# Attention weights transposed in 32x32 blocks by VectorE and placed by SBUF transfers

## The reference

```python
u = einsum('bsd,dc->bsc', rmsnorm(x, g), w_in)       # q, k, v, gates of three branches
ya = forgetting_attention(qa, ka, va, log_f) * silu(za)   # 4 heads, causal, decay bias
yb = dilated_mixture_attention(rope(qb), rope(kb), vb) * silu(zb)   # 6 heads
yc = banded_attention(rope(qc), rope(kc), vc, 127, sinks) * silu(zc) # 6 query, 2 kv heads
merged = sigmoid(ga)*(ya@w_br_a) + sigmoid(gb)*(yb@w_br_b) + sigmoid(gc)*(yc@w_br_c)
x = x + merged @ w_out
```

## Time and profile before

| | us |
|---|---|
| median of 3 runs | 2319.72 |
| lowest and highest | 2318.62, 2319.8 |
| profiled execution | 2318.26 |
| its span, first to last instruction | 2316.5 |
| TensorE busy | 2300.3 (99%) |
| VectorE busy | 1282.9 (55%) |
| ScalarE busy | 855.2 (37%) |

### The profile page before, as it was taken

The page is one execution under the profiler, slowest core; times in us unless marked ns, Lnnn a source line. Parts: engine busy times, 40 slices in busy tenths (PEclk is TensorE's granted clock), DMA queues, the critical chain, the costliest instruction groups (busy, mean ns, idle before and its releaser), DMA issues.

```text
span 2316.5 us, 28465 instructions
## 1 busy us (share of the span) xinstructions
PE 2300.3 (99%) x11494; PEld 1877.6 (81%) x11494; DVE 1282.9 (55%) x2217; ACT 855.2 (37%) x1419; POOL 13.9 (1%) x14
## 2 busy tenths in 40 slices
PE   9999999999999999999999999999999999999998
PEld 7787778878777787878889888888888888888887
DVE  5855565556656556586545544444755546444445
ACT  5334443433444334354334432232322334332233
POOL 0000000000000000200000000000000000000000
PEclk9999999999999999999999999999999999999999
DMA  4322222322322233324224222222222212222221
GB/s 174 93 87 86 80 78 99 105 78 92 91 82 76 82 102 109 121 70 139 91 82 129 99 92 97 95 92 99 91 93 99 91 46 92 99 91 99 92 93 63
DMA packets 67271, 218.23 MB, mean 94 GB/s; under 512 B 8479, under 2 KB 11167, under 8 KB 67012
## 3 DMA queue, kind: packets, MB, share of 16 engines
q1 hardware_dynamic: 67140, 216.41, 28.2%
HBM read 209.02 MB, written 3.42 MB: 92 GB/s over the span
## 4 chain that ended last, share of the span: by engine, by line
PE 96%; DVE 2%; ACT 1%; POOL 0%; issue 0%; DMA 0%; SPq 0%; POOLq 0%; DVEq 0%; ACTq 0%
PE ps L370 27%; PE ps L372 27%; PE ps L371 27%; PE ps L573 2%; PE ps L661 2%; PE ps L396 2%; PE ps L397 2%; PE ps L398 2%; PE ps L641 1%; PE ps L1457 1%; PE ps L1407 1%; PE ps L462 1%; POOL t_UP L170 0%; PE ps L923 0%; PE ps L921 0%; PE ps L922 0%
## 5 line engine op out<-in xcount | busy, mean ns | idle before, releaser
L370 PE MATMUL ps<-t_P0H,t_whi 128*128 128x512 f32 x1664 | 670.8, 403 | 1.9 <-DVE t_P0L L176 1.9
L372 PE MATMUL ps<-t_P0H,t_wlo 128*128 128x512 f32 x1664 | 655.8, 394 | 0.0
L371 PE MATMUL ps<-t_P0L,t_whi 128*128 128x512 f32 x1664 | 654.6, 393 | 0.0
L182 ACT ACTIVATE t_whi<-t_raw 128x1024 fp32r<-128x1024 f32 (+3 forms) x395 | 404.9, 1029 | 418.8 <-PE ps L372 346.4
L173 DVE TENSOR_TENSOR t_wlo<-t_raw,t_whi 128x1024 fp32r<-128x1024 f32 (+3 forms) x394 | 468.1, 1188 | 52.5 <-PE ps L398 35.0
L370 PEld LDWEIGHTS ps<-t_P0H,t_whi 128*128 128x128 f32 x1664 | 313.2, 188 | 93.7 <-issue 23.0
L372 PEld LDWEIGHTS ps<-t_P0H,t_wlo 128*128 128x128 f32 x1664 | 312.6, 188 | 72.9
L371 PEld LDWEIGHTS ps<-t_P0L,t_whi 128*128 128x128 f32 x1664 | 313.1, 188 | 69.7 <-issue 2.4
L370 PE MATMUL ps<-t_P1H,t_whi 128*128 128x512 f32 (+1 forms) x932 | 361.3, 388 | 0.3 <-DVE t_P1L L173 0.3
L371 PE MATMUL ps<-t_P1L,t_whi 128*128 128x512 f32 (+1 forms) x932 | 359.5, 386 | 0.0
L372 PE MATMUL ps<-t_P1H,t_wlo 128*128 128x512 f32 (+1 forms) x916 | 355.6, 388 | 0.0
(11 more groups left out here) (241 smaller groups left out, 2403.5 us busy)
## 6 DMA issues: line engine op xcount, KB each, us to landing
t_raw<-in_wts SPq DMA_DIRECT2D x362, 512.0 KB, 3.4
t_raw<-in_wts SPq DMA_DIRECT2D x16, 384.0 KB, 3.0
t_raw<-in_wts SPq DMA_DIRECT2D x13, 256.0 KB, 2.7
t_raw<-in_wts SPq DMA_DIRECT2D x4, 520.0 KB, 4.9
t_X<-in_xT SPq DMA_DIRECT2D x8, 256.0 KB, 5.6
t_TMX<-t_TMX SPq DMA_DIRECT2D x28, 64.0 KB, 2.0
t_TMP<-t_TMX SPq DMA_DIRECT2D x24, 64.0 KB, 2.0
outT<-t_X SPq DMA_DIRECT2D x4, 384.0 KB, 2.6
```

The lines of the kernel that those rows point to most:

```text
L182: return lambda e: e.activation(o, a, f, **k)
L370: e.matmul(bank[:, 0:N], wh, xh, start=first, stop=False)
L371: e.matmul(bank[:, 0:N], wh, xl, start=False, stop=False)
L372: return e.matmul(bank[:, 0:N], wl, xh, start=False, stop=end)
```

## The change

In the first block turn is replaced by turn_by_dma. VectorE transposes all 32x32 blocks of a head's weights in one instruction and writes them sorted, so that for every partition group i the blocks that belong to partition group j lie side by side. Twelve transfers issued by SP move the blocks with i and j different (32 partitions, 192 or 256 values each), and ScalarE copies the four with i = j. Both heads of a unit share these. The products read the operand as four runs of 32 and lag the scores by three units instead of two. Each stage lends one buffer more for the sources (a part of M or QKV that is idle then). The two banks of the transposes become score banks, four in all; TB shrinks to two buffers, the temporaries to nine; two semaphores more are there for the transfers.

```diff
-NRAW, NHI, NLO, NTMP, NTMX = 4, 4, 3, 5, 5
+NRAW, NHI, NLO, NTMP, NTMX = 4, 4, 3, 5, 4
...
-    SB = Turns([ps[:, b, :] for b in (3, 4)])
-    PTP = Turns([ps[:, 5, :]])
+    SB = Turns([ps[:, b, :] for b in (3, 4, 5)])
+    PTP = Turns([])
...
-    TB = Turns([T["Tb"][:, i, :] for i in range(3)] + [T["TbX"][:, 0, :]])
-    PTS = Turns([T["PTb"][:, i, :] for i in range(2)])
+    TB = Turns([T["Tb"][:, 0, :], T["TbX"][:, 0, :]])
+    PTS = Turns([])
...
+    blocks = Turns([wide(T["Tb"][:, 1:3, :])])
+    turned = Turns([wide(T["PTb"][:, :, :]), wide(T["PTX"][:, :, :])])
+    moved = [0]
...
+        def turn_by_dma(u):
+            kh = u["cols"] // 128
+            run_ = 2 * kh * 32
+            src, sfree = blocks.take()
+            s4 = src[:, 0:4 * run_].rearrange("p (j k b) -> p j k b", j=4, b=32)
+            o = None
+            for h, (t, ready) in enumerate(u["P"]):
+                o = op(DV, lambda e, h=h, t=t: e.transpose(
+                    s4[:, :, h * kh:(h + 1) * kh, :].rearrange("p j k b -> p k j b"),
+                    t[:, 0:128 * kh].rearrange("p (k j b) -> p k j b", j=4, b=32)), ready, sfree if h == 0 else None)
+                TB.give(t, o)
+            dst, dfree = turned.take()
+            n, sem = moved[0] // 2, T["s_t"][moved[0] % 2]
+            moved[0] += 1
+            landed, count = None, 0
+            for i in range(4):
+                for j in range(4):
+                    if i == j:
+                        continue
+                    count += 1
+                    landed = Q.dma(SP, lambda e, i=i, j=j: e.dma_start(
+                        dst[32 * j:32 * j + 32, i * run_:(i + 1) * run_],
+                        src[32 * i:32 * i + 32, j * run_:(j + 1) * run_]), sem, 16 * (12 * n + count), o, dfree)
+            own = [op(AC, act(dst[32 * i:32 * i + 32, i * run_:(i + 1) * run_],
+                              src[32 * i:32 * i + 32, i * run_:(i + 1) * run_], ACT.Copy), o, dfree) for i in range(4)]
+            blocks.give(src, landed, own[-1])
+            d4 = dst[:, 0:4 * run_].rearrange("p (i k b) -> p i k b", i=4, b=32)
+            u["PT"] = [landed, own[-1]]
+            u["cut"] = [lambda k, h=h: d4[:, :, h * kh + k // 128, :] for h in range(2)]
+            u["held"] = dst
...
-                            i = e.matmul(held[b][0][base:base + rows, 128 * q:128 * q + 128], vs[k][j],
-                                         pts[m][:, o + 128 * j:o + 128 * j + 128],
+                            out = held[b][0][base:base + rows, 128 * q:128 * q + 128]
+                            i = e.matmul(out.rearrange("p (a b) -> p a b", a=4), vs[k][j], cut[m](o + 128 * j),
...
+        if by_dma:
+            for i in range(n + 3):
+                if i >= 3:
+                    values(units[i - 3])
+                if 1 <= i <= n:
+                    norm(units[i - 1])
+                    turn_by_dma(units[i - 1])
+                if i < n:
+                    scores(units[i])
+                for _ in range(2):
+                    yield
+                    flush()
+            return
...
-            PTP.idle += [x for x in G.idle if x[0] is spare[1]]
+            SB.idle += [x for x in G.idle if x[0] is spare[1]]
...
+        phase("forget", tok, 2, qA, kA, vA, [0, 1], [0, 1], gens_B(tokB), 90, 18, M[:, 4:6, :])
+        phase("mix", tokB, 3, qB, kB, vB, [2, 3, 4], [2, 3, 4], gens_C(tokC), 138, 24, QKV[:, 4:6, :])
+        phase("sink", tokC, 3, qC, kC, vC, [5, 0, 1], [0, 1, 2], gens_D(), 112, 18, QKV[:, 6:8, :])
```

More of the change, by code:

```diff
@@ L153, in lay_out, with wide @@
     G = Turns([ps[:, b, :] for b in (0, 1, 2)] + spare)
-    SB = Turns([ps[:, b, :] for b in (3, 4)])
-    PTP = Turns([ps[:, 5, :]])
+    SB = Turns([ps[:, b, :] for b in (3, 4, 5)])
+    PTP = Turns([])
     OB = Turns([])
-    TB = Turns([T["Tb"][:, i, :] for i in range(3)] + [T["TbX"][:, 0, :]])
-    PTS = Turns([T["PTb"][:, i, :] for i in range(2)])
+    TB = Turns([T["Tb"][:, 0, :], T["TbX"][:, 0, :]])
+    PTS = Turns([])
+    def wide(ap):
+        return ap.rearrange("p a b -> p (a b)")
+    blocks = Turns([wide(T["Tb"][:, 1:3, :])])
+    turned = Turns([wide(T["PTb"][:, :, :]), wide(T["PTX"][:, :, :])])
+    moved = [0]
     TMP = Turns([T["TMP"][:, i, :] for i in range(NTMP)] + [T["TMX"][:, i, :] for i in range(NTMX)])
@@ L556, in residual, with attention @@
         return make
-    def attention(units, done_pair, late_values=False):
+    def attention(units, done_pair, late_values=False, by_dma=False):
         st = {}
@@ L654, in values @@
             held = st["O"]
-            pts = [pt for pt, _ in u["PT"]]
+            if by_dma:
+                cut, ready = u["cut"], u["PT"]
+            else:
+                cut = [lambda k, pt=pt: pt[:, k:k + 128].rearrange("p (a b) -> p a b", a=4) for pt, _ in u["PT"]]
+                ready = [a for _, a in u["PT"]]
             def f(e):
@@ L660, in f @@
                         for b, base, rows, vs, m in u["outs"]:
-                            i = e.matmul(held[b][0][base:base + rows, 128 * q:128 * q + 128], vs[k][j],
-                                         pts[m][:, o + 128 * j:o + 128 * j + 128],
+                            out = held[b][0][base:base + rows, 128 * q:128 * q + 128]
+                            i = e.matmul(out.rearrange("p (a b) -> p a b", a=4), vs[k][j], cut[m](o + 128 * j),
                                          start=j == 0, stop=j == n // 128 - 1)
                 return i
-            p = op(PE, f, [a for _, a in u["PT"]], u["vtok"], *[x[1] for x in held] if u["first"] else [])
-            for pt in pts:
-                PTS.give(pt, p)
+            p = op(PE, f, ready, u["vtok"], *[x[1] for x in held] if u["first"] else [])
+            if by_dma:
+                turned.give(u["held"], p)
+            else:
+                for pt, _ in u["PT"]:
+                    PTS.give(pt, p)
             if u["last"]:
@@ L1033, in lay_out, with phase @@
         tokB, tokC = {}, {}
[L1034 to L1039, removed]
+        def phase(kind, tk, npair, q, k, v, slots, zslots, fill, num, den, more):
+            blocks.idle.append((wide(more), [f for _, f in turned.idle if f]))
+            drive(attention(units(kind, tk, npair, q, k, v), gate_y(slots, zslots, ztok), by_dma=True), fill, num, den)
+            blocks.idle = [x for x in blocks.idle if x[0].tensor.name == T["Tb"][:, 0, :].tensor.name]
+            assert len(blocks.idle) == 1 and len(turned.idle) == 2
+            drain()
+        phase("forget", tok, 2, qA, kA, vA, [0, 1], [0, 1], gens_B(tokB), 90, 18, M[:, 4:6, :])
+        phase("mix", tokB, 3, qB, kB, vB, [2, 3, 4], [2, 3, 4], gens_C(tokC), 138, 24, QKV[:, 4:6, :])
+        phase("sink", tokC, 3, qC, kC, vC, [5, 0, 1], [0, 1, 2], gens_D(), 112, 18, QKV[:, 6:8, :])
         crow = [(64 * i, 64 * (i + 3)) for i in range(3)]
@@ L1083, in lay_out @@
     TB.idle = [b for b in TB.idle if b[0].tensor.name == T["Tb"][:, 0, :].tensor.name]
-    assert len(TB.idle) == 3 and len(PTP.idle) == 2
-    OB.idle += PTP.idle[1:]
-    PTP.idle = PTP.idle[:1]
+    TB.idle += [(T["Tb"][:, i, :], blocks.idle[0][1]) for i in (1, 2)]
+    PTS.idle = [(T["PTb"][:, i, :], [f for _, f in turned.idle]) for i in range(2)]
+    assert len(TB.idle) == 3 and len(SB.idle) == 4 and len(OB.idle) == 1
+    PTP.idle, SB.idle = SB.idle[:1], SB.idle[1:]
+    OB.idle, SB.idle = OB.idle + SB.idle[:1], SB.idle[1:]
     N.gtok = None
@@ L1751, in tensors @@
                  ("LC", [128, 512]), ("MC", [128, 256]), ("tri", [128, 128]),
-                 ("fg", [128, 5, 16]), ("TMX", [128, NTMX, 512]), ("TbX", [128, 1, 512])):
+                 ("fg", [128, 5, 16]), ("TMX", [128, NTMX, 512]), ("TbX", [128, 1, 512]), ("PTX", [128, 2, 512])):
         put(n, s)
@@ L1790, in build_program @@
         T["s_r"] = [sem(f"s_r{i}") for i in range(3)]
+        T["s_t"] = [sem(f"s_t{i}") for i in range(2)]
         sems = {e: sem("s_" + e) for e in (PE, DV, AC, PO, SP)}
```

## The result

| | median us | runs |
|---|---|---|
| before | 2319.3 | 5 |
| changed | 2328.14 | 5 (2327.78 to 2330.79) |

The ratio is 1.004 (95% interval 1.0025 to 1.0055): the change makes the kernel slower by 0.4%, 9 us. I had forecast 2313, faster. The span of the profiled execution is 2326.4 us, 9.9 more than before.

The account below looks back on a forecast made before the run. TensorE, busy 99% of the span, was taken as the bound. 2318.3 - 31.2 (transposes) + 2 x (11.6 forget + 0.5 mix) = 2311.3, plus 1.4 from profiled execution to median: 2313 us, range 2291 to 2332.

Parts of the forecast that it names:

- The removed transposes: All attention stages: 284 fewer TensorE transposes save 15.6 us a layer (forget 4.4, mix 6.6, sink 4.6), 31.2 in all.
- The products' new operand: TensorE's products read four runs of 32 at no extra cost; bounds 0 and +16 us.
- The block transposes: VectorE: 84 transposes at 0.6 us each, 50 us in all, leaving VectorE below TensorE in forget.
- An issue: SP's queue: each transfer takes 0.625 us to issue, 7.5 us per unit of twelve; bounds 5.7 and 8.9.
- rival A: SP keeps up at 0.47 us a transfer, forget and mix lose little; 2291 us, chance 0.22.
- Sink: Sink stage: SP has 7.5 + 0.8 of 9.8 us and no swaps, so 0 lost; removed transposes save 4.6 a layer.
- B: SP's issues cost 0.74 us, losing 22.6 us in forget and 12 in mix per layer; 2358 us, chance 0.13.
- C: VectorE becomes the bound through dear block transposes in forget, mix and sink; 2378 us, chance 0.03.
- D: Strided operands slow TensorE's products, +16 us on the forecast; 2329 us, chance 0.09.
- The term of forget: Forget stage: SP's queue falls behind and late transfers delay the last products, +11.6 us a layer; bounds 9.3 to 14.
- The term of mix: Mix stage: SP keeps up in total; a landing made late by VectorE's stops costs 0.5 us a layer, bounds 0 and 4.
- The clock: TensorE's clock lowered by a long stall: not in the forecast, 0 to 3 us a layer left in the high end.

Follow-up runs that it names:

- the third experiment: The changed kernel with the additions of the rotary swaps recorded five flushes after the projection instead of three: 2320.72 us, ratio 1.0005.
- the stall experiment: The kernel before with one stall in each of its six attention stages, by two or four GpSimd additions: 2343.25 and 2360.95 us.

## Why the prediction was wrong

**Right.** The removed transposes: forget falls to 74.5 and 74.8 when SP is light (four transfers), 74.6 forecast. The products' new operand costs nothing: in the changed kernel the first come 12 in 0.81 us (78.28 to 79.09), the time of the earlier trace rows. The block transposes take

```profile
L648 DVE STREAM_TRANSPOSE t_Tb<-t_Tb 128x384 f32<-128x384 f32 x16 | 9.2, 572 | 0.0
L648 DVE STREAM_TRANSPOSE t_Tb<-t_Tb 128x512 f32<-128x512 f32 x6 | 4.2, 705 | 0.0
```

0.57 and 0.71 us where I took 0.6. An issue costs SP 0.625, as taken from the earlier trace rows, and SP's queue bounds the forget stage; rival A is out by that row, though its 2291 is nearly the 2292 of four transfers, by luck: it had SP at 0.47 for all twelve. Sink, with what follows it up to the next layer: -4.3 in layer 1, -4.6 forecast. B, C and D have no part in it: issues are not dearer, VectorE is not full, the products keep their pace.

**The term of forget, mis-sized: 14.5 us over the undisturbed 74.6 instead of 11.6.** SP began 1.2 us later than I had put it and its queue broke off a little more often: the last products, which wait for the last landing, began 82.2 us after the start instead of 78.7, 3.5 us. The stalls also lay elsewhere than I said (1 to 2 us at unit 3, 7 at unit 4, 2 at unit 5): 2.1 at unit 2, 4.8 at unit 3, 0.9 at unit 4 and 1.8 at unit 5. I had written that VectorE's stops could only reach TensorE through score banks. That was the step that failed. There is one output bank and there are three projection banks, and VectorE frees these too. In forget it made next to no difference to the end, as the third experiment shows (88.8 and 88.5 against 89.1).

**The term of mix, mis-sized: 4.8 and 5.8 us instead of 0.5.** Same step: the stops of up to 6.8 us reached TensorE through the projection banks, in one wait of 2.75 us in layer 1 and one of 2.15 in layer 2. With the additions later or the swaps elsewhere, mix is 114.6; the stops cost 3.0 and 4.0 us, in layer 2 with up to 1.7 of lowered clock. The rest to 112.8, 1.8 us, stays with all of these edits, and with four transfers too: one wait of 1.4 us for a projection bank. So it isn't from the late swaps. I take it for VectorE's added work there (10 us of block transposes in the stage); that was not tested. Of the 17 us between the forecast span and the measured one, mix has 9.6 and forget 5.8.

**The clock, left to the high end at 0 to 3 us a layer.** No row of the kernel before showed it. It did fall, but it explains only about a third of the loss. Two lowered stretches of the first forget stage and the one behind them, in windows (columns as above):

```profile
99.00:102.40 3.40, 3.40 (x15) 1.47 (x11) 0.20 (x1) 2.18 (x4) 0.00 (x0) 0.50 0.45 95
112.60:119.50 6.90, 5.44 (x30) 5.11 (x31) 6.54 (x15) 2.89 (x7) 0.00 (x0) 0.51 0.64 202
119.50:123.00 3.50, 3.50 (x32) 3.50 (x31) 3.50 (x6) 1.77 (x3) 0.00 (x0) 1.00 0.18 46
```

The same 128x256 matmuls start 0.21 us apart up to 119.3 and 0.12 apart from 119.5 on. Lowered stretches: 3.4 and 6.8 us in layer 1, both in forget; 6.8 in forget and 3.4 in mix of layer 2; a fifth of 3.4 in the second block. Of these 23.9 us TensorE worked some 19.6, which at full clock take half, 9.8 us less. That this is nearly the loss of 9.9 is chance, for most of it cost nothing. In forget TensorE worked 4.4 us longer than with four transfers in layer 1 (78.8 against 74.4) and 2.4 in layer 2 (76.8 against 74.4), and both stages last 89.1. After the lowered stretches it still waited for the transfers of the last two units, 0.9 and 1.8 us in layer 1, 0.8 and 2.7 in layer 2: at full clock it would have come to these waits earlier and waited longer. What is left is the stretch in mix and the one in the second block, at most 1.7 us each, some 3 us in all. Without them the waits would still have eaten more than the 31.2 us of the transposes.

The Trainium skill, "TensorE: Matmul & The Clock Gate", section "Why this matters for your kernels", warns against idle gaps between matmuls because the clock falls behind them. The trace agrees: in the stall experiment the granted clock is 0.50 for 3.4 us or more behind each of the twelve.

The fifth stretch is chance: the second block has the same wait before and after (2.4 us for a ScalarE copy, at 1008 and 1017), and only in the second profile the clock fell after it.

**Added up** (us against before, span): transposes -31.2; forget, by SP's queue, 2 x 14.5 = +29.0; mix +10.6, of it 7.0 by VectorE's stops (with the clock of one stretch) and 3.6 that stays without them; the rest +1.7, mostly the stretch in the second block. That is +10.1 for the measured +9.9.

**The range and the rivals.** 2328 lies within 2291 to 2332, and within the forecast's own extremes of 2307 to 2330, but partly by luck. Forget lost more than its bound of 14 and mix more than its bound of 4; the 3 us a layer kept for the clock covered them, and the clock cost about half of that. 2332 was meant for rival D, and D did not happen. In rival B's sum one figure is wrong: at 0.68 an issue, its own terms for mix give 108 against 104, 4 us lost and not 1, so 2330 and not 2324.

## What to carry to other kernels

Before work moves from TensorE to many small transfers, add up the issuing engine's time per stage (here 0.625 us each) against the stage's length, all its other DMAs included: 63 us of queue, which can start only at 13 and must land before the last products are due at 67, was too much; 48 cost 1.5 to 3 us. List for each engine that may now stand still every buffer that it frees, not only the one of the new step. And price a TensorE stall of some us above its length, here 1.4 to 2 us more each, but only where nothing behind it waits for a slower queue anyway: there the lowered clock cost nothing.

## What was not expected of the hardware

- ScalarE and SP issue at the same time at nearly full pace (0.613 and 0.590 each), but an issue on ScalarE is ScalarE's time: six a unit undid the gain.
- GpSimd issues the swaps in 0.496 us, less than SP (0.590), with the same 2.0 us to landing.
- The granted clock fell after all twelve stalls that were put in (2.8 to 6.0 us from start to start). In the changed kernel it fell after one of 2.5 us (95.9) and not after one of 3.15 (206.8), and in the profile of the kernel before not after the 2.8 us of the second block, where in the changed kernel's it did. A stall's length alone doesn't settle it; what else does, these runs don't tell.
